# Moving x's fourth tile and the sample rows behind the first quarter of the modulation, and the gates' weights behind the last, in a one-layer hybrid decoder step

## The chip, the cores and the metric

The kernel runs on one core of a Trainium2 chip. The metric is the device time of one execution in microseconds (us); the time of the kernel before is the median of three runs. Engines are named as in the profile: PE is TensorE (PEld its weight loads), DVE is VectorE, ACT is ScalarE, POOL is GpSimd, SP is SyncE, which here only issues transfers.

## What is computed

One layer over 512 prompt rows and 64 sample rows (8 sequences of 8) of width 1024. Only its head matters here. Everything is float32.

```python
mod = silu(c) @ w_mod + b_mod                 # c: 1 prompt row and 8 sample rows; w_mod: 1024 x 6144
sh1, sc1, g1, sh2, sc2, g2 = split(mod, 6)
u = rmsnorm(x, n_pre1) * (1 + sc1) + sh1      # 576 rows
z = u @ w_in                                  # 1024 x 3072: xr, yg, q, k, v, g
...                                           # RG-LRU on xr (its gates: w_rgate, w_igate), retention on q, k, v
x = x + g1 * rmsnorm(concat(out_a, out_b) @ w_out, n_post1)
...                                           # router, 16 experts, second residual
```

## The kernel before, in words

Each engine runs its own instruction stream, written out by hand; semaphores join them. There is no scheduler: what stands ahead in an engine's stream is done first, and a wait holds up all that stands behind it.

**Tokens and tiles.** The 576 rows are five tiles t of x: 0 to 3 are 128 prompt rows each, 4 is the 64 sample rows. Each tile is squared and summed on ACT (`Square`, then `Sqrt`), scaled on DVE (`norm_x`: a reciprocal and a multiplication into `xn`), turned by PE in eight 128-column pieces into two PSUM banks (`turn_x`, line 741), and copied to `uT` (features on partitions, 8 slices k of 128 features by 576 tokens) by `take_x` on ACT (slices 0 to 3) and on DVE (slices 4 to 7).

**Scale and shift.** `1 + sc1` and `sh1` are needed per feature. They are made in four quarters q of 256 features (two slices k each). For a quarter, `scale_part(q, 0)` and `scale_part(q, 1)` on PE multiply the nine conditioning rows by two 1 MB pieces of `w_mod`, spread over four groups of 32 rows; ACT copies the first result to `part`, DVE the second; `scale_sum(q, 0)` and `(q, 1)` on PE (rows `con,arena 128x32`) add up the groups with `part` as the stationary operand; DVE makes `scaleT` from it (lines 1811, 1812, 1814) and raises `s_scaled`. Then ACT scales slice 2q of `uT` over the 512 prompt tokens (`s_uTa`), DVE slice 2q+1 (line 1821) and the sample columns of both slices (lines 1825 and 1826), raising `s_uTd` for each.

**First products.** `first_tile(q, n, m)` adds quarter q's share (slices 2q and 2q+1) to output tile m (0 to 2) of the first 512 columns of `w_in`, for token half n: 0 is tokens 0 to 287, 1 is tokens 288 to 575. It writes bank 2+2m+n. Six tiles and two parts of the next quarter make up one quarter of PE's stream; in the loop over q the next quarter's `scale_part` stand between the first three tiles and the last three, and its `scale_sum` between `first_tile(q, 1, 0)` and `(q, 1, 1)`, so that the ACT and DVE steps of a quarter lie beside products of the quarter before.

**Transfers.** SP issues, in this order: the four prompt tiles of x (512 KB each), the sample rows (256 KB), then for each quarter two pieces of `w_mod` (1 MB each, `load`, line 499) and 512 KB of `w_in` (`load_first`, line 505; it first waits until ACT has squared tile q), then the other pieces into a ring of nine 1 MB slots, each when PE has used up what the slot held. POOL issues small parameters, waits until PE has done four scale parts, issues the gates' weights (`wgate`, four transfers of 64 KB with rows of 256 bytes, line 577), waits for eight, and issues biases, norms and the rest of the constants. `wgate` is first read by `gate_products(0)`, after the 24 first tiles and `by_channel(0, 3)`.

```python
            for q in range(3):
                for m in range(3):
                    first_tile(q, 0, m)
                scale_part(q + 1, 0)
                scale_part(q + 1, 1)
                first_tile(q, 1, 0)
                scale_sum(q + 1, 0)
                scale_sum(q + 1, 1)
                first_tile(q, 1, 1)
                first_tile(q, 1, 2)
```

## Time and profile before

| | us |
|---|---|
| median of three runs | 573.47 (573.0 to 574.8) |
| the profiled execution's own time | 574.29 |
| its span in the profile | 572.3 |
| PE busy | 550.2 (96%) |
| DVE, ACT, POOL busy | 212.0 (37%), 166.4 (29%), 98.5 (17%) |

The span runs from the first instruction to the last; some 2 us lie around it. All times below are counted from the span's start. A busy share says little by itself: what counts is which engine waits, where, and for whom.

### The profile page before, as it was taken

Reading aid. Unit: us, or ns where it says so; the run is one execution under the profiler, and the core shown is the slowest. Engines: PE = TensorE matmul, PEld = TensorE weight load, DVE = VectorE, ACT = ScalarE, POOL = GpSimd, SP = SyncE. Lnnn points to the kernel's source line nnn. Section 1 sums busy time; section 2 is a strip of 40 time slices with the busy share of each in tenths; the row PEclk is TensorE's granted clock in tenths of the full one; section 3 lists DMA queues with packets and bytes.
Section 4 is the critical chain, followed back from the end, with each engine's and each line's share of the span. In section 5 each row is a group of like instructions: output and inputs, shape, how many; then the busy total and the mean of one; then the engine's idle time right before and its main releaser. Section 6 shows DMA issues by size and latency. Waiting matters only on the chain.

```text
span 572.3 us, 6747 instructions
## 1 busy us (share of the span) xinstructions
PE 550.2 (96%) x2562; PEld 341.4 (60%) x2562; DVE 212.0 (37%) x526; ACT 166.4 (29%) x326; POOL 98.5 (17%) x116
## 2 busy tenths in 40 slices
PE   7899999999999999999999999799999999999984
PEld 6577755544454555574444455677777777777641
DVE  3434386421232233325433656422223223221137
ACT  7332676712123122322323343111112112111142
POOL 3016000133000000003100211313232422232110
PEclk8999999999999999999999999999999999999998
DMA  8999997899300000089400359969999999999564
GB/s 278 356 332 338 333 351 318 296 389 340 133 1 0 0 1 1 1 286 350 118 37 37 111 177 314 274 229 340 338 326 344 354 349 332 331 354 344 125 203 166
DMA packets 73492, 133.15 MB, mean 233 GB/s; under 512 B 4138, under 2 KB 49618, under 8 KB 71410
## 3 DMA queue, kind: packets, MB, share of 16 engines
q1 hardware_dynamic: 58864, 99.36, 50.3%
q0 software_dynamic: 9536, 28.75, 18.1%
q10 hardware_dynamic: 5058, 4.58, 2.4%
q8 instruction: 22, 0.36, 0.3%
q14 instruction: 12, 0.10, 0.0%
HBM read 117.47 MB, written 18.35 MB: 237 GB/s over the span
## 4 chain that ended last, share of the span: by engine, by line
PE 87%; DVE 5%; DMA 4%; ACT 2%; issue 1%; ACTq 0%; SPq 0%
PE psum L717 82%; PE psum L720 4%; DMA ring<-in_w_mod_dram 2%; DMA out_dram<-arena 1%; DVE arena L2203 1%; ACT arena L1365 1%; DVE x L2207 1%; DMA hy<-in_c_sample_dram 1%; DVE arena L2044 0%; ACT L1365 0%; DVE arena L2125 0%; DVE arena L2258 0%; ACT ss L1365 0%; ACTq L1605 0%; ACT hy L1365 0%
## 5 line engine op out<-in xcount | busy, mean ns | idle before, releaser
L717 PE MATMUL psum<-ring,arena 128*128 128x256 f32 (+1 forms) x640 | 173.5, 427 | 1.8 <-DVE arena L2258 1.3
L717 PEld LDWEIGHTS psum<-ring,arena 128*128 128x128 f32 x640 | 120.3, 192 | 38.8 <-issue 25.8
L717 PE MATMUL psum<-ring,uT 128*128 128x512 f32 (+1 forms) x384 | 126.5, 522 | 0.0
L1365 ACT ACTIVATE arena<-psum 128x512 f32<-128x512 f32 (+6 forms) x111 | 50.7, 478 | 229.8 <-PE psum L717 202.8
L717 PEld LDWEIGHTS psum<-ring,uT 128*128 128x128 f32 (+1 forms) x384 | 56.5, 172 | 60.1 <-issue 55.8
L717 PE MATMUL psum<-uT,ring 128*128 128x288 f32 x256 | 64.9, 410 | 1.3 <-ACT uT L1365 1.3
L717 PEld LDWEIGHTS psum<-uT,ring 128*128 128x128 f32 x256 | 47.7, 190 | 17.5 <-issue 5.1
L720 PEld LDWEIGHTS psum<-con,arena 128*128 128x128 f32 (+1 forms) x295 | 35.5, 145 | 21.4 <-issue 14.1
L720 PE MATMUL psum<-con,arena 128*128 128x128 f32 (+1 forms) x295 | 42.2, 280 | 4.1 <-DVE arena L2303 3.1
L2303 DVE TENSOR_TENSOR arena<-arena,psum 128x256 f32<-128x256 f32 x16 | 6.7, 421 | 98.5 <-ACT arena L1365 98.5
L1365 ACT ACT_TABLE_LOAD x33 | 42.3, 1283 | 3.1 <-issue 2.1
L717 PE MATMUL psum<-arena 128*128 128x128 f32 (+5 forms) x188 | 35.0, 367 | 0.9 <-issue 0.7
L717 PE MATMUL psum<-ring,hy 128*128 128x512 f32 (+1 forms) x80 | 32.9, 600 | 0.5 <-ACT arena L1365 0.5
L717 PE MATMUL psum<-ring,outbT 128*128 128x512 f32 (+1 forms) x80 | 32.4, 593 | 0.0
L664 POOL DMA_INDIRECT arena<-u_dram,slot_tok x16 | 17.1, 1068 | 76.5 <-DVE slot_tok L2184 76.2
L717 PEld LDWEIGHTS psum<-arena 128*128 128x128 f32 (+3 forms) x188 | 21.3, 178 | 12.4 <-issue 10.6
L692 POOL DMA_INDIRECT f_dram<-arena,add_tok x15 | 23.9, 1596 | 18.1 <-issue 12.9
L2267 DVE TENSOR_SCALAR arena<-psum,arena 128x512 f32<-128x512 f32 x15 | 11.3, 751 | 41.7 <-PE psum L717 41.7
L1365 ACT ACTIVATE arena<-psum,con 128x128 f32<-128x128 f32 x36 | 10.4, 367 | 53.1 <-PE psum L717 46.2
L1365 ACT ACTIVATE arena<-psum,arena 128x512 f32<-128x512 f32 x15 | 10.3, 687 | 47.5 <-PE psum L717 47.5
L717 PE MATMUL psum<-ring,rowsT 128*32 128x256 f32 (+1 forms) x256 | 22.8, 490 | 0.8 <-DMA ring<-in_w_mod_dram 0.7
L717 PEld LDWEIGHTS psum<-ring,outbT 128*128 128x128 f32 (+1 forms) x80 | 13.2, 179 | 17.2 <-issue 17.2
(214 smaller groups left out, 421.8 us busy)
## 6 DMA issues: line engine op xcount, KB each, us to landing
ring<-in_w_mod_dram SPq DMA_DIRECT2D x24, 1024.0 KB, 11.4
ring<-in_w_exp_gate_dram SPq DMA_DIRECT2D x16, 1024.0 KB, 10.9
ring<-in_w_exp_up_dram SPq DMA_DIRECT2D x16, 1024.0 KB, 16.6
ring<-in_w_exp_down_dram SPq DMA_DIRECT2D x16, 1024.0 KB, 11.7
ring<-in_w_in_dram SPq DMA_DIRECT2D x10, 1024.0 KB, 14.3
ring<-in_w_out_dram SPq DMA_DIRECT2D x4, 1024.0 KB, 14.9
f_dram<-in_consts_dram POOLq DMA_DIRECT2D x1, 3072.0 KB, 20.5
arena<-in_state_ret_dram POOLq DMA_DIRECT2D x6, 512.0 KB, 5.4
```

The lines of the kernel that those rows point to most:

```text
L664: pool.indirect_dma_start(out=xg[e % 2], out_offset=None, in_=u2_dram, in_offset=bass.IndirectOffsetOnAxis(ap=slot_tok[:, e:e + 1], axis=0))\
L692: pool.indirect_dma_start(out=f_dram, in_=eo[e % 2], in_offset=None, compute_op=ALU.add, out_offset=bass.IndirectOffsetOnAxis(ap=add_tok[: ...
L717: return nc.tensor.matmul(out, lhsT, rhs, start=first, stop=last)
L720: return nc.tensor.transpose(out, src, ident[0:src.shape[0], 0:src.shape[0]])
L1365: return nc.scalar.activation(out, src, func, **kw).then_inc(done, 1)
L2203: v.scalar_tensor_tensor(out=Y[:, t, 0:w], in0=src[:, 0:w], scalar=ss[:, 3, t, 0:1], in1=tab["g2" + tag(t)][:, 0:w], op0=ALU.mult, op1=ALU ...
L2207: v.tensor_tensor(out=x[:, t, 0:w], in0=x[:, t, 0:w], in1=Y[:, t, 0:w], op=ALU.add)\
L2267: v.tensor_scalar(eo[e % 2][:, 512:1024], bank[5], gsl[e % 2][:, e:e + 1], None, ALU.mult).then_inc(s_eod, 1)
L2303: v.tensor_tensor(out=hg[e % 2], in0=hb[e % 2], in1=bank[e % 2][:, FE:2 * FE], op=ALU.mult).then_inc(s_hm, 1)
```

## The change

- SP issues tiles 0 to 2 of x, quarter 0's two pieces of `w_mod`, then tile 3 and the sample rows, then the first quarter of `w_in` and the rest as before.
- ACT and DVE norm, scale and take tiles 0 to 2 first; tile 3 and the sample rows (t = 3 and 4) are normed after quarter 0's scale is applied to tokens 0 to 383, and then taken and scaled over tokens 384 to 511 in instructions of their own. ACT takes all eight slices of the sample rows.
- PE does quarter 0's first three tiles (token half 0), then turns tiles 3 and 4, and does `scale_part(1, 0)` after `first_tile(0, 1, 0)`, and `scale_part(1, 1)` and both sums of quarter 1 after `first_tile(0, 1, 2)`. Quarters 2 and 3 keep their order.
- POOL issues the gates' weights after eight scale parts, ahead of the biases.

```diff
--- before.py
+++ after.py
@@ -507,14 +507,18 @@
                              w_in[0, q * 2 * P:(q + 1) * 2 * P, 0:512]
                              .rearrange("(k p) n -> p k n", p=P)).then_inc(s_xt[q], 16)
-            for t in range(TILES - 1):
+            def load_x(t):
                 sp.dma_start(x[:, t, :], x_prompt[0, t * P:(t + 1) * P, :]).then_inc(s_xt[t], 16)
-            sp.dma_start(x[0:NS, TILES - 1, :], x_sample.rearrange("b t d -> (b t) d"))\
-                .then_inc(s_xt[TILES - 1], 16)
-
+
+            for t in range(TILES - 2):
+                load_x(t)
             for q in range(4):
                 load(("scale", q, 0))
                 load(("scale", q, 1))
+                if q == 0:
+                    load_x(TILES - 2)
+                    sp.dma_start(x[0:NS, TILES - 1, :], x_sample.rearrange("b t d -> (b t) d"))\
+                        .then_inc(s_xt[TILES - 1], 16)
                 load_first(q)
             for p in weight_pieces():
                 if p[0] != "scale" and p[:2] != ("in", 0) and p not in late:
@@ -570,13 +574,12 @@
             pool.dma_start(brow[16:24, :], norm_pre_mix[0].rearrange("(r n) -> r n", n=P))\
                 .then_inc(s_par, 16)
-            pool.wait_ge(s_scale, 4)
+            pool.wait_ge(s_scale, 8)
             for gi, w in enumerate((w_rgate, w_igate)):
                 wv = w[0].rearrange("(m a) j k -> a j m k", a=2)
                 for a in range(2):
                     pool.dma_start(wgate[64 * a:64 * a + 64, gi, :, :], wv[a]).then_inc(s_par, 16)
-            pool.wait_ge(s_scale, 8)
             pool.wait_ge(s_clear, 3)
             for j in range(4):
                 pool.dma_start(bm[32 * j:32 * j + 32, :, :],
@@ -741,11 +744,14 @@
                 n = rows(t)
                 pe.wait_ge(s_xn, t + 1)
                 if t >= 3:
-                    pe.wait_ge(s_rawa, t - 2)
-                    pe.wait_ge(s_rawd, t - 2)
-                b = 2 + 2 * (t % 3)
+                    pe.wait_ge(s_rawd, t - 1)
                 for k in range(KT):
-                    at = bank[b + k // 4][:, (k % 4) * P:(k % 4) * P + n]
+                    if t < 3:
+                        at = bank[2 + 2 * t + k // 4][:, (k % 4) * P:(k % 4) * P + n]
+                    elif t == 3:
+                        at = bank[3 + 2 * (k // 4)][:, (k % 4) * P:(k % 4) * P + n]
+                    else:
+                        at = bank[7][:, k * n:(k + 1) * n]
                     last = turn(at, xn[0:n, t, k * P:(k + 1) * P])
                 last.then_inc(s_uTp, 1)
@@ -777,10 +783,8 @@
             turn_x(2)
             turn_rows()
             scale_part(0, 0)
-            turn_x(3)
+            scale_sum(0, 0)
             scale_part(0, 1)
-            turn_x(4)
-            scale_sum(0, 0)
             scale_sum(0, 1)
             half = NTOK // 2
@@ -813,18 +817,30 @@
                 w = ring[:, slot["in", 0, q // 2], :].rearrange("p (k n) -> p k n", n=512)
                 if m == 0 and n == 0:
                     pe.wait_ge(s_xt[q], 32)
-                    pe.wait_ge(s_uTa, q + 1)
+                    pe.wait_ge(s_uTa, q + 1 + (q > 0))
                 if m == 0 and n == 1:
-                    pe.wait_ge(s_uTd, 2 * q + 2)
+                    pe.wait_ge(s_uTa, q + 2)
+                    pe.wait_ge(s_uTd, 2 * q + 3)
                 for k in (2 * q, 2 * q + 1):
                     if m == 0 and n == 0 and k % 2 == 1:
-                        pe.wait_ge(s_uTd, 2 * q + 1)
+                        pe.wait_ge(s_uTd, 2 * q + 1 + (q > 0))
                     last = mm(bank[2 + 2 * m + n][:, 0:half], w[:, k % 4, m * P:(m + 1) * P],
                               uT[:, k, n * half:(n + 1) * half], k == 0, k == KT - 1)
                 if q == 3 and n == 1:
                     last.then_inc(s_xr, 1)
-            for q in range(3):
+            for m in range(3):
+                first_tile(0, 0, m)
+            turn_x(3)
+            turn_x(4)
+            first_tile(0, 1, 0)
+            scale_part(1, 0)
+            first_tile(0, 1, 1)
+            first_tile(0, 1, 2)
+            scale_part(1, 1)
+            scale_sum(1, 0)
+            scale_sum(1, 1)
+            for q in (1, 2):
                 for m in range(3):
                     first_tile(q, 0, m)
                 scale_part(q + 1, 0)
@@ -1377,33 +1393,50 @@
             def take_x(t):
                 n = rows(t)
                 act.wait_ge(s_uTp, t + 1)
-                b = bank[2 + 2 * (t % 3)][:].rearrange("p (k i) -> p k i", i=P)
-                f(uT[:, 0:4, t * P:t * P + n], b[:, :, 0:n], ACT.Copy, s_rawa)
-
-            for t in range(TILES):
+                if t < TILES - 1:
+                    b = bank[2 + 2 * t if t < 3 else 3][:].rearrange("p (k i) -> p k i", i=P)
+                    f(uT[:, 0:4, t * P:t * P + n], b[:, :, 0:n], ACT.Copy, s_rawa)
+                else:
+                    b = bank[7][:].rearrange("p (k i) -> p k i", i=n)
+                    f(uT[:, :, t * P:t * P + n], b, ACT.Copy, s_rawa)
+
+            def size_x(t):
                 n = rows(t)
                 act.wait_ge(s_xt[t], 16)
                 f(xn[0:n, t], x[0:n, t], ACT.Square, s_sq, accum_out=ss[0:n, 0, t, 0:1])
                 act.wait_ge(s_sq, t + 1)
                 f(ss[0:n, 0, t, 0:1], ss[0:n, 0, t, 0:1], ACT.Sqrt, s_xrms, scale=1.0 / D,
                   bias=eps[0:n, 0:1])
-                if t >= 2:
-                    take_x(t - 2)
+
+            size_x(0)
+            size_x(1)
+            size_x(2)
+            take_x(0)
+            take_x(1)
+            take_x(2)
+
+            def times_scale(k, tokens):
+                f(uT[:, k, tokens], uT[:, k, tokens], ACT.Identity, s_uTa,
+                  scale=scaleT[:, 0, k, 0:1], bias=scaleT[:, 1, k, 0:1])
             def scale_u(q):
                 act.wait_ge(s_scale, 2 * q + 1)
                 if q:
                     act.wait_ge(s_scaleT, 2 * q)
                 f(part[:, 0, 0:256], bank[0][:, 0:256], ACT.Copy, s_parta)
-                if q == 0:
-                    take_x(TILES - 2)
-                    take_x(TILES - 1)
                 act.wait_ge(s_scaled, q + 1)
-                if q == 0:
-                    act.wait_ge(s_rawa, TILES)
-                    act.wait_ge(s_rawd, TILES)
-                f(uT[:, 2 * q, 0:SEQ], uT[:, 2 * q, 0:SEQ], ACT.Identity, s_uTa,
-                  scale=scaleT[:, 0, 2 * q, 0:1], bias=scaleT[:, 1, 2 * q, 0:1])
+                if q:
+                    times_scale(2 * q, slice(0, SEQ))
+                    return
+                act.wait_ge(s_rawa, 3)
+                act.wait_ge(s_rawd, 3)
+                times_scale(0, slice(0, 3 * P))
+                size_x(3)
+                size_x(4)
+                take_x(3)
+                take_x(4)
+                act.wait_ge(s_rawa, TILES)
+                times_scale(0, slice(3 * P, SEQ))
             scale_u(0)
             scale_u(1)
@@ -1783,7 +1816,7 @@
             def take_x(t):
                 n = rows(t)
                 dve.wait_ge(s_uTp, t + 1)
-                b = bank[3 + 2 * (t % 3)][:].rearrange("p (k i) -> p k i", i=P)
+                b = bank[3 + 2 * t if t < 3 else 5][:].rearrange("p (k i) -> p k i", i=P)
                 v.tensor_copy(uT[:, 4:KT, t * P:t * P + n], b[:, :, 0:n]).then_inc(s_rawd, 1)
             norm_x(0)
@@ -1791,10 +1824,8 @@
             take_x(0)
             norm_x(2)
             take_x(1)
-            norm_x(3)
             take_x(2)
             take_rows()
-            norm_x(4)
             def scale_u(q):
@@ -1802,24 +1833,36 @@
                 of = lambda j: bank[j][:, 0:64].rearrange("p (k r) -> p k r", r=32)[:, :, 0:1 + DB]
                 wide = lambda r: r.unsqueeze(2).to_broadcast([P, 2, 1 + DB])
                 a, b = scaleT[:, 0, two, 0:1 + DB], scaleT[:, 1, two, 0:1 + DB]
-                dve.wait_ge(s_scale, 2 * q + 2)
-                v.tensor_copy(part[:, 1, 0:256], bank[1][:, 0:256]).then_inc(s_partd, 1)
-                if q == 0:
-                    take_x(TILES - 2)
-                    take_x(TILES - 1)
+                if q:
+                    dve.wait_ge(s_scale, 2 * q + 2)
+                    v.tensor_copy(part[:, 1, 0:256], bank[1][:, 0:256]).then_inc(s_partd, 1)
                 dve.wait_ge(s_scaleT, 2 * q + 1)
                 link(v.tensor_tensor(out=a, in0=of(0), in1=wide(biasT[:, 1, two]), op=ALU.add))
                 link(v.tensor_tensor(out=a, in0=a, in1=wide(biasT[:, 2, two]), op=ALU.mult))
+                if q == 0:
+                    dve.wait_ge(s_scale, 2)
+                    v.tensor_copy(part[:, 1, 0:256], bank[1][:, 0:256]).then_inc(s_partd, 1)
                 dve.wait_ge(s_scaleT, 2 * q + 2)
                 v.tensor_tensor(out=b, in0=of(1), in1=wide(biasT[:, 0, two]), op=ALU.add)\
                     .then_inc(s_scaled, 1)
                 dve.wait_ge(s_scaled, q + 1)
+                k = 2 * q + 1
+
+                def times_scale(tokens):
+                    v.tensor_scalar(uT[:, k, tokens], uT[:, k, tokens], scaleT[:, 0, k, 0:1],
+                                    scaleT[:, 1, k, 0:1], ALU.mult, ALU.add).then_inc(s_uTd, 1)
+
                 if q == 0:
-                    dve.wait_ge(s_rawd, TILES)
+                    dve.wait_ge(s_rawd, 3)
+                    dve.wait_ge(s_rawa, 3)
+                    times_scale(slice(0, 3 * P))
+                    norm_x(3)
+                    norm_x(4)
+                    take_x(3)
                     dve.wait_ge(s_rawa, TILES)
-                k = 2 * q + 1
-                v.tensor_scalar(uT[:, k, 0:SEQ], uT[:, k, 0:SEQ], scaleT[:, 0, k, 0:1],
-                                scaleT[:, 1, k, 0:1], ALU.mult, ALU.add).then_inc(s_uTd, 1)
+                    times_scale(slice(3 * P, SEQ))
+                else:
+                    times_scale(slice(0, SEQ))
                 each = lambda j: scaleT[:, j, two, 1:1 + DB].unsqueeze(3).to_broadcast([P, 2, DB, DT])
                 u = uT[:, two, SEQ:NTOK].rearrange("p k (b t) -> p k b t", t=DT)
                 link(v.tensor_tensor(out=u, in0=u, in1=each(0), op=ALU.mult))
```

PE's stream from quarter 0's first scale part to quarter 1's first products. Names: `ring,rowsT 32x256` are scale parts (x8 is one), `con,arena 128x128` and `128x64` the turns of a prompt tile and of the sample rows, `con,arena 128x32` the sums (x2 is one), `uT,ring 128x288` first tiles (x2 is one). Before:

```order
L717 MATMUL psum<-ring,rowsT 32x256 x8
L720 MATMUL psum<-con,arena 128x128 x8
L717 MATMUL psum<-ring,rowsT 32x256 x8
L720 MATMUL psum<-con,arena 128x64 x8
L717 MATMUL psum<-con,arena 128x32 x4
L717 MATMUL psum<-uT,ring 128x288 x6
L717 MATMUL psum<-ring,rowsT 32x256 x16
L717 MATMUL psum<-uT,ring 128x288 x2
L717 MATMUL psum<-con,arena 128x32 x4
L717 MATMUL psum<-uT,ring 128x288 x10
```

And in the changed kernel:

```order
L720 MATMUL psum<-con,arena 128x32 x2
L720 MATMUL psum<-ring,rowsT 32x256 x8
L720 MATMUL psum<-con,arena 128x32 x2
L720 MATMUL psum<-uT,ring 128x288 x6
L723 MATMUL psum<-con,arena 128x128 x8
L723 MATMUL psum<-con,arena 128x64 x8
L720 MATMUL psum<-uT,ring 128x288 x2
L720 MATMUL psum<-ring,rowsT 32x256 x8
L720 MATMUL psum<-uT,ring 128x288 x4
L720 MATMUL psum<-ring,rowsT 32x256 x8
L720 MATMUL psum<-con,arena 128x32 x4
L720 MATMUL psum<-uT,ring 128x288 x6
```

The turns moved from before the sums to behind three first tiles, quarter 1's parts moved behind `first_tile(0, 1, 0)` and `(0, 1, 2)`, and its sums from between the products to behind them all.

ACT's stream over the same stretch (`arena,ss<-x` is a tile's square, `ss<-ss,eps` its root, `uT<-psum` take_x, `arena<-psum 128x256` the copy of a part, `uT<-uT,scaleT` the scaling of a slice). Before:

```order
L1365 ACTIVATE uT<-psum 128x4x128 [waits s_uTp]
L1365 ACTIVATE arena,ss<-x 64x1024 [waits s_xt4]
L1365 ACTIVATE ss<-ss,eps 64x1 [waits s_sq]
L1365 ACTIVATE uT<-psum 128x4x128 [waits s_uTp]
L1365 ACTIVATE arena<-psum 128x256 [waits s_scale]
L1365 ACTIVATE uT<-psum 128x4x128 [waits s_uTp]
L1365 ACTIVATE uT<-psum 128x4x64 [waits s_uTp]
L1365 ACTIVATE uT<-uT,scaleT 128x512 [waits s_rawd,s_rawa,s_scaled]
L1365 ACTIVATE arena<-psum 128x256 [waits s_scaleT,s_scale]
L1365 ACTIVATE uT<-uT,scaleT 128x512 [waits s_scaled]
```

And in the changed kernel:

```order
L1381 ACTIVATE uT<-psum 128x4x128 [waits s_uTp] x3
L1381 ACTIVATE arena<-psum 128x256 [waits s_scale]
L1381 ACTIVATE uT<-uT,scaleT 128x384 [waits s_rawd,s_rawa,s_scaled]
L1381 ACTIVATE arena,ss<-x 128x1024 [waits s_xt3]
L1381 ACTIVATE ss<-ss,eps 128x1 [waits s_sq]
L1381 ACTIVATE arena,ss<-x 64x1024 [waits s_xt4]
L1381 ACTIVATE ss<-ss,eps 64x1 [waits s_sq]
L1381 ACTIVATE uT<-psum 128x4x128 [waits s_uTp]
L1381 ACTIVATE uT<-psum 128x8x64 [waits s_uTp]
L1381 ACTIVATE uT<-uT,scaleT 128x128 [waits s_rawa]
L1381 ACTIVATE arena<-psum 128x256 [waits s_scaleT,s_scale]
L1381 ACTIVATE uT<-uT,scaleT 128x512 [waits s_scaled]
```

The squares and takes of tiles 3 and 4 moved from ahead of the first scaling to behind it, and the copy of quarter 1's first part now stands behind all of them.

## Rows read from the trace of the kernel before

**Rows 1.** The page, part 4: the chain that ended last, shares of the span by engine.

```profile
PE 87%; DVE 5%; DMA 4%; ACT 2%; issue 1%; ACTq 0%; SPq 0%
```

**Rows 2.** The chain in order of time: start, length, what.

```profile
26.36 90.77 PE psum L717 x540
```

**Rows 3.** Timeline, PE and PEld: start, length, engine, line, what, [idle before <-releaser].

```profile
7.90 0.66 PE L720 MATMUL psum<-con,hy 9*128 9x9 f32 x8 [1.56 <-DMA con<-in_consts_dram]
...
15.31 1.07 PE L717 MATMUL psum<-ring,rowsT 128*32 128x256 f32 x16
...
16.31 1.09 PE L720 MATMUL psum<-con,arena 128*128 128x128 f32 x8
...
18.47 0.71 PE L720 MATMUL psum<-con,arena 64*128 64x64 f32 x8
...
19.11 1.08 PE L717 MATMUL psum<-con,arena 128*128 128x32 f32 x8
...
21.47 3.15 PE L717 MATMUL psum<-uT,ring 128*128 128x288 f32 x12 [1.28 <-ACT uT L1365]
...
26.36 1.07 PE L717 MATMUL psum<-ring,rowsT 128*32 128x256 f32 x16 [0.74 <-DMA ring<-in_w_mod_dram]
...
27.36 1.24 PE L717 MATMUL psum<-uT,ring 128*128 128x288 f32 x4
...
29.25 5.10 PE L717 MATMUL psum<-uT,ring 128*128 128x288 f32 x20
...
34.27 2.01 PE L717 MATMUL psum<-ring,rowsT 128*32 128x256 f32 x32
...
35.21 0.59 PEld L717 LDWEIGHTS psum<-ring,rowsT 128*32 128x32 f32 x16 [0.35 <-DMA ring<-in_w_mod_dram]
...
62.57 2.17 PE L717 MATMUL psum<-arena,wgate 64*64 64x512 f32 x16
```

**Rows 4.** Timeline, ACT and DVE, same columns.

```profile
12.51 1.05 ACT L1365 ACTIVATE arena<-x 128x1024 f32<-128x1024 f32 x1
...
13.68 0.29 ACT L1365 ACTIVATE ss<-ss,eps 128x1 f32<-128x1 f32 x1
...
14.27 0.75 DVE L1780 TENSOR_SCALAR arena<-x,ss 128x1024 f32<-128x1024 f32 x1
...
15.72 0.57 ACT L1365 ACTIVATE uT<-psum 128x512 f32<-128x512 f32 x1
...
18.61 0.42 DVE L1806 COPY arena<-psum 128x256 f32<-128x256 f32 x1 [1.48 <-PE psum L717]
...
19.88 0.17 DVE L1811 TENSOR_TENSOR scaleT<-psum,rowsT 128x18 f32<-128x18 f32 x1
...
20.51 0.82 ACT L1365 ACTIVATE uT<-uT,scaleT 128x512 f32<-128x512 f32 x1 [0.91 <-DVE scaleT L1814]
...
21.29 0.29 DVE L1826 TENSOR_TENSOR uT<-uT,scaleT 128x128 f32<-128x128 f32 x1
...
29.73 0.81 ACT L1365 ACTIVATE uT<-uT,scaleT 128x512 f32<-128x512 f32 x1 [3.66 <-DVE scaleT L1814]
```

**Rows 5.** Two-microsecond windows: busy of each engine, granted clock, DMA share, GB/s.

```profile
10.00:12.00 2.00, 1.99 (x10) 1.99 (x11) 0.92 (x2) 1.64 (x5) 0.00 (x0) 0.50 1.11 256
20.00:22.00 2.00, 0.72 (x4) 0.57 (x4) 1.44 (x6) 0.82 (x1) 0.00 (x0) 1.00 1.11 351
32.00:34.00 2.00, 2.00 (x10) 1.52 (x8) 1.14 (x7) 1.55 (x3) 0.00 (x0) 1.00 1.11 273
34.00:36.00 2.00, 2.00 (x34) 0.83 (x32) 0.78 (x6) 0.38 (x1) 0.00 (x0) 1.00 1.07 244
```

**Rows 6.** Tile ring, SP, from 28.7 us: scale piece (3, 1), issue to landing.

```profile
L499 SPq DMA_DIRECT2D ring<-in_w_mod_dram x1: 3318/3318/3318, 28.7 to 28.7; - x1
...
DMA to landing us min/median/max: 14.2/14.2/14.2
```

**Rows 7.** The page, part 6 and the DMA view: the gates' weights, median us to landing.

```profile
wgate<-in_w_rgate_dram POOLq DMA_DIRECT2D x2, 64.0 KB, 5.8
```


## The prediction

> **What bounds the kernel now.** First the chain of waits by engine: 87% of the span is PE, 4% DMA [rows 1]. Then the same chain in order of time: from 26.36 us on it is PE's own stream, 540 instructions without a foreign step [rows 2]. So past 26.36 a microsecond of PE idle time, added or removed, goes to the end, unless a transfer or another engine stands in between. Third, the timeline of PE around the change: what bounds it there is read from the brackets. After quarter 0's sums PE idles 1.28 us until ACT has scaled the first slice, and 0.74 us at 26.36 until piece (1, 1) of w_mod has landed [rows 3]. The next piece that it waits for is (2, 1), and that wait shows only on the weight load, 0.35 us at 35.21 [rows 3]. Piece (3, 1) lands at 28.7 + 14.2 = 42.9 us [rows 6], before PE reads it (PE comes to it one quarter, some 9 us, after 35.21). So up to 26.36 transfers set the pace, and from there PE is just barely ahead of being held by them.
>
> The DMA engines are full there (share over 1, 351 GB/s), and at 32 to 36 us they carry only 273 and 244 GB/s [rows 5]: that is when the gates' weights land, issued from 27.8 us in rows of 256 bytes, 5.8 us to landing [rows 7].
>
> **The change, part by part.** The anchor is the start of first_tile(1, 0, 0). Before, the 20 records from 29.25 us are five first tiles of 1.02 us each (5.10 / 5) [rows 3], of which two belong to quarter 0: it starts at 29.25 + 2.04 = 31.3 us. From it on both kernels have the same order on PE.
>
> *Start.* Tiles 0 to 2 are loaded, normed and turned as before; quarter 0's part (0, 0) again starts at 15.31, behind the turned parameter rows, for 1.07 us [rows 3]. Its weights had come by then even with 768 KB more ahead of them.
>
> *Quarter 0's scale.* Part (0, 0) ends at 16.4; the copy (like DVE's, 0.42 us [rows 4]) to 16.9; the first sum takes PE half of 1.08 us, to 17.4; part (0, 1) to 18.5 [rows 3]. DVE's copy, 0.42 us, to 19.0; the sum starts at 19.1. Before, DVE read a sum 0.77 us after its start (19.11 to 19.88), and ACT's scaling began 0.63 us later, behind three DVE instructions of some 0.2 us each [rows 3, 4]; now two of the three are done earlier. So ACT starts at 19.1 + 0.8 + 0.2 = 20.1, not 20.51. It scales 384 columns: 512 took 0.82 us, I take 0.65. First products at 20.8 instead of 21.47 us: 0.7 won.
>
> *Tiles 3 and 4, now in the open.* Three first tiles, 3.15 us [rows 3], end at 23.95. Beside them ACT squares tile 3 (20.75; root 1.17 us later, as 12.51 to 13.68, and 0.29 long) and tile 4 (22.1; root ends at 23.6); DVE's reciprocal and multiplication (0.15 + 0.75) give tile 4 at 24.6 [rows 4]. Up to here all is hidden. Then PE turns tile 3 (1.09 us, the next may start after 0.85) and tile 4 (0.71) [rows 3], ending at 25.5. What follows is on the path, since first_tile(0, 1, 0) waits for both: ACT takes tile 3 (0.57) from 25.1 and tile 4, now eight slices, 512 columns, also 0.57, from 25.7, to 26.3 [rows 4]; then DVE, which waits for ACT here, scales 128 columns (0.25, from 0.55 for 512) and does the two sample instructions, 0.29 each [rows 4]. That is 27.2; PE resumes at 27.3 after 1.8 us of idle time. Before, first_tile(0, 1, 0) started at 27.36 [rows 3]. The two kernels are level there, but before had already done parts (1, 0) and (1, 1), and now both still stand ahead.
>
> *Quarter 1's scale, in the open too.* first_tile(0, 1, 0) 1.02, part (1, 0) 0.95 (34.27 to 35.21, one part behind the other [rows 3]), two first tiles 2.04, part (1, 1) 1.07: 27.3 + 5.1 = 32.4 us. All of w_mod it needs landed by 26.3. Now nothing is left of quarter 0 to lie beside the handing over: DVE's copy from 32.45 to 32.9, the second sum 0.8 to 33.7, line 1814 0.2, ACT's scaling of 512 columns 0.81 (29.73 [rows 4]): 34.7, and PE at 34.8 us. Of those 2.4 us PE works about 1.0 on the sums. Before, scaling ended at 30.54 and PE came to it at 31.3: hidden whole.
>
> So the anchor moves from 31.3 to 34.8: **+3.5 us**. Back comes what PE lost at 35.21 to piece (2, 1): two parts took 2.01 us [rows 3] against 2 x 0.95, so 0.1. Sum: **+3.4 us**.
>
> *The gates' weights.* Away from 32 to 36 us they free the DMA engines: 4 us at a mean of 258 GB/s instead of 351 [rows 5] is 0.37 MB not moved, and 0.26 MB of what was moved was theirs, together 0.63 MB or 1.8 us for pieces (3, 1) and what follows, some 1.3 us for (2, 1), which was landing. But with PE at 37.9 us for part (2, 0), (2, 1) landed before 35.2 and (3, 1) before 42.9, no transfer is waited for: worth nothing. The Trainium skill, DMA: Bandwidth & Descriptors, Why small descriptors are slow, gives a 256-byte descriptor 27% overhead; by that the 256 KB would cost about 1.0 us and not 1.8, an estimate by that page. It changes neither term above. Later the four issues, 0.65 us each by the issue times, start when PE has done eight parts, at about 48.8, ahead of the biases; with 5.8 us to landing [rows 7], and 10 as a bound for fuller queues, they land by 62. They are read at 62.57 + 3.4 = 66 us [rows 3]. The biases and norms slip 3 us and are read after the first eight mod steps, tens of microseconds later.
>
> *The rest of the kernel* is PE's stream, its transfers released by PE itself, and so moves as a whole.
>
> Against the median of 573.47, +3.4 gives **576.9 us** (the profiled execution was 574.29, span 572.3: those would be 577.7 and 575.7). The unknowns: the 384-, 128- and 512-column instructions that the trace lacks, and some ten handoffs of 0.05 to 0.1 us; 0.9 us either way. A measurement tells about 0.3%, 1.7 us, from no change.
>
> **Rivals.**
>
> *Transfers go on setting the pace, and PE is not late (not slower).* If the copies and scalings overlapped so well that quarter 0's last tiles ran before 26.3 us, part (1, 1) would start on its landing as before, and the three first tiles that followed it would be done. Then (2, 1) is the next wait, and it lands up to 1.3 us earlier without the gates' weights: 572.2 us. For it: PE did wait at 26.36 and 35.21 for just these pieces. Against: it decides if first_tile(0, 1, 0) starts before 22.3 us (three tiles and part (1, 0) ahead of 26.3), and PE ends only the first three tiles at 23.95, with work it cannot drop. A half of it, in which the two open handoffs shrink by 1.5 to 2 us together, ends near 575. I give 12% to results under 575.2, of which 3% to a gain over 1.7 us.
>
> *The clock.* After 1.56 us of idle time at 6.34 to 7.90 and then only small turns, the granted clock was 0.50 over 10 to 12 us, which is 1.2 GHz; at 20 to 22 us, with PE busy 0.72 of 2 us, it stayed at 1.00, 2.4 GHz [rows 3, 5]. The new gaps of 1.8 and 1.4 us stand between dense work, as the latter did. If one did lower it for 3.5 us, as around 9 to 13, half of that is lost: 1.75 more, 578.7 us. The Trainium skill, TensorE: Matmul & The Clock Gate, HAM oscillation, names such idle gaps between loads as what halves the clock; its example's gaps are longer than these, and beyond the two rows above no row shows what a gap as short as these does. This case has 8%.
>
> *The gates' weights come too late.* If they took as long as the constants that now stand behind them, near 18 us, they would land at 69.5, and PE would stand 3.5 us more at 66: 580.4 us. Against: they are first in POOL's queue. 3%.
>
> **How the numbers follow.** The forecast, 77%: 575.2 to 577.9. Under 575.2: 12%. The clock 8%, the weights 3%. The range from 574.6 to 578.7 leaves out about 6% below and 7% above. Slower by over 0.3%: 77 + 8 + 3 = 88%, less 2 for the forecast's own edge, 86%; within 0.3%: 11%; faster: 3%.
>
> **What would show it.** Right: PE's first products start near 20.8; an idle time near 1.8 us before first_tile(0, 1, 0) at 27.3, ended by DVE's sample instruction; one of some 1.4 us before first_tile(1, 0, 0) at 34.8, ended by ACT's scaling; parts (2, 0) and (2, 1) at 37.9 with no wait on a transfer; the gate products at 66. Wrong: quarter 1's part (1, 1) before 28 us; a granted clock under 1.00 after 13 us; a wait on `wgate`; or parts of quarter 2 still waiting for w_mod, which would mean that transfers, and not the order, set the pace.

## The result, and the profile after

| | before | changed |
|---|---|---|
| median of four runs each, us | 574.13 (573.00 to 574.85) | 581.72 (577.85 to 583.61) |
| profiled execution, its span | 574.29, 572.3 | 577.85, 575.9 |

The medians lie 7.6 us apart (1.3%); the ratio on record is 1.0098, with an interval from 1.0066 to 1.013, which is 5.6 us. By either the change is slower, by 1.7 to 2.2 times the 3.4 us forecast, and the median is outside the range. The profiled execution was the quickest of the changed kernel's four, and 0.95 us from the forecast. So two things want explaining: what this trace shows, and what the three other executions, at 581.4 to 583.6, had besides. The mean granted clock gives the first hint: 0.990 in the profiled one, and 0.987, 0.985 and 0.982 in those of 581.4, 582.05 and 583.6 us.

The page of the changed kernel: busy time by engine, chain by engine.

```profile
PE 550.0 (96%) x2562; PEld 341.1 (59%) x2562; DVE 212.1 (37%) x526; ACT 167.8 (29%) x327; POOL 98.2 (17%) x116
...
PE 86%; DVE 6%; DMA 5%; ACT 1%; issue 1%; ACTq 0%; POOLq 0%; DVEq 0%
```

PE is as busy as before (550.0 against 550.2 us) and its share of the chain is about the same, 86% against 87% [rows 1]: no work was added. Its place in time changed: it waited more (below), and where the clock was low the same products took longer. The timeline of PE (start, length, engine, line, operation, tiles, count, idle time before and what ended it) answers to [rows 3]:

```profile
14.72 1.07 PE L720 MATMUL psum<-ring,rowsT 128*32 128x256 f32 x16
...
18.54 0.63 PE L720 MATMUL psum<-con,arena 128*128 128x32 f32 x4 [0.62 <-DVE arena L1844]
...
20.28 4.84 PE L720 MATMUL psum<-uT,ring 128*128 128x288 f32 x12 [1.11 <-ACT uT L1381]
...
28.33 1.21 PE L720 MATMUL psum<-uT,ring 128*128 128x288 f32 x4 [1.69 <-DVE uT L1869]
...
29.46 1.07 PE L720 MATMUL psum<-ring,rowsT 128*32 128x256 f32 x16
...
32.60 1.07 PE L720 MATMUL psum<-ring,rowsT 128*32 128x256 f32 x16
...
36.14 3.15 PE L720 MATMUL psum<-uT,ring 128*128 128x288 f32 x12 [1.28 <-ACT uT L1381]
...
39.21 1.93 PE L720 MATMUL psum<-ring,rowsT 128*32 128x256 f32 x32
```

And ACT and DVE, answering to [rows 4]:

```profile
19.43 0.71 ACT L1381 ACTIVATE uT<-uT,scaleT 128x384 f32<-128x384 f32 x1 [3.19 <-DVE scaleT L1846]
...
27.31 0.50 ACT L1381 ACTIVATE uT<-uT,scaleT 128x128 f32<-128x128 f32 x1
...
27.89 0.29 DVE L1869 TENSOR_TENSOR uT<-uT,scaleT 128x128 f32<-128x128 f32 x1
...
35.17 0.82 ACT L1381 ACTIVATE uT<-uT,scaleT 128x512 f32<-128x512 f32 x1 [4.19 <-DVE scaleT L1846]
```

The gap structure is the predicted one: 1.69 us of idle time ahead of first_tile(0, 1, 0), ended by DVE's sample instruction (predicted 1.8), and 1.28 us ahead of first_tile(1, 0, 0), ended by ACT's scaling (predicted 1.4); parts (2, 0) and (2, 1) without a wait on a transfer. The first products began at 20.28, 0.5 us ahead of the forecast, because part (0, 0) had itself started at 14.72 and not at 15.31; from that part to the products it is 5.6 us, where 5.5 was reckoned. But the first products took 4.84 us for the same 12 records that took 3.15 [rows 3], and with these 1.69 us more (4.84 less 3.15) first_tile(1, 0, 0) starts at 36.14 instead of 34.8. Two-microsecond windows (busy of PE, PEld, DVE, ACT, POOL, granted clock, DMA share, GB/s) say why; a granted clock of 1.00 is 2.4 GHz, 0.50 is 1.2 GHz, and values between are windows in which it changed:

```profile
19.00:21.00 2.00, 0.89 (x5) 0.71 (x5) 0.66 (x2) 1.57 (x3) 0.00 (x0) 1.00 1.11 350
21.00:23.00 2.00, 2.00 (x7) 1.36 (x6) 1.01 (x3) 1.81 (x6) 0.00 (x0) 0.56 1.08 345
23.00:25.00 2.00, 2.00 (x7) 1.38 (x6) 0.81 (x2) 0.00 (x0) 0.00 (x0) 0.59 1.07 373
25.00:27.00 2.00, 1.64 (x17) 1.33 (x15) 0.69 (x1) 0.92 (x2) 0.00 (x0) 1.00 1.10 350
```

At 21 to 25 us the granted clock is 0.56 and 0.59: it fell to 1.2 GHz at 21.2 and came back at 24.6. Before it fell, in 19 to 21 us, PE was busy 0.89 of 2 us. In the kernel before, with 0.72 busy in 20 to 22, it had stayed at 1.00 [rows 5]. The gate products came at 67.4 us, 4.8 later than before [rows 3], but the end only 3.6 later: in the kernel before the clock also fell at 371 us, behind the 2.2 us gap ahead of the first expert's turn, and in this execution of the changed kernel it did not. PE before:

```profile
369.45 0.44 PE L720 MATMUL psum<-con,arena 128*128 128x128 f32 x2 [2.21 <-DVE arena L2303]
370.25 8.83 PE L717 MATMUL psum<-ring,arena 128*128 128x256 f32 x32 [0.36 <-DVE arena L2258]
```

and in the changed kernel:

```profile
374.94 7.14 PE L720 MATMUL psum<-ring,arena 128*128 128x256 f32 x32 [0.37 <-DVE arena L2301]
```

So past 13 us each of the two profiled executions lost about 1.7 us to one such stretch (4.84 against 3.15, 8.83 against 7.14), the changed kernel at 21 us and before at 371. The two cancel, and the 3.6 us that are left are the order. That this execution came out beside the forecast is therefore luck in part: the forecast held neither stretch.

### The profile page after: what moved, and what is told of

Same layout as the page of the kernel before. It is cut to its first block, busy times and chain, and to the rows that moved or that the text cites. A ratio compares the mean times of both kernels' runs of the same rounds, so it can differ in the third digit from the quotient of the medians.

```text
span 575.9 us, 6751 instructions
## 1 busy us (share of the span) xinstructions
PE 550.0 (96%) x2562; PEld 341.1 (59%) x2562; DVE 212.1 (37%) x526; ACT 167.8 (29%) x327; POOL 98.2 (17%) x116
## 4 chain that ended last, share of the span: by engine, by line
PE 86%; DVE 6%; DMA 5%; ACT 1%; issue 1%; ACTq 0%; POOLq 0%; DVEq 0%
PE psum L720 80%; PE psum L723 5%; DMA f_dram<-arena,add_tok 2%; DMA out_dram<-arena 1%; DVE arena L2246 1%; DMA con<-in_consts_dram 1%; DVE x L2250 1%; DMA arena<-f_dram 1%; ACT arena L1381 1%; ACT uT L1381 0%; DVE arena L2087 0%; DVE arena L2168 0%; DVE arena L2375 0%; DVE arena L2301 0%; ACTq L1638 0%
## 5 line engine op out<-in xcount | busy, mean ns | idle before, releaser
L720 PEld LDWEIGHTS psum<-ring,arena 128*128 128x128 f32 x640 | 119.1, 190 | 38.3 <-issue 25.8
L720 PE MATMUL psum<-uT,ring 128*128 128x288 f32 x256 | 66.9, 418 | 4.1 <-ACT uT L1381 2.4
L720 PE MATMUL psum<-ring,outbT 128*128 128x512 f32 (+1 forms) x80 | 32.4, 593 | 0.0
L720 PEld LDWEIGHTS psum<-arena 128*128 128x128 f32 (+3 forms) x188 | 21.2, 178 | 12.8 <-issue 10.6
L684 POOL DMA_INDIRECT arena<-gates_dram,slot_tok x15 | 14.5, 970 | 49.3 <-DVE arena L2310 22.2
```

The source lines that it names most:

```text
L684: pool.indirect_dma_start(out=gsl[e % 2], out_offset=None, in_=gates_dram, in_offset=bass.IndirectOffsetOnAxis(ap=slot_tok[:, e:e + 1], ax ...
L720: return nc.tensor.matmul(out, lhsT, rhs, start=first, stop=last)
```

## The experiments

All ran with the kernel before beside them on the same chip. Its median there was 575.2, 574.8 and 575.5 us in the three sets, with executions from 571.5 to 578.7: wider than the first runs had shown. "Filler" means a product of the identity matrix with 128 columns (itself or a table of constants) into PSUM columns that nobody reads, in a place where PE is idle anyway. Theory C is that the new order costs what was forecast and that the clock's falls are the rest. Theory O is that the order is all, and the rest is scatter.

**1. The changed kernel again (after_again)**, with no edit.

> The changed kernel once more, in the same runs as the others. Theory C (the new order of PE costs some 3 us, and the gaps it opens before 29 us let the granted clock fall to 0.50 once more, 1.7 us each time): the median stays 577 to 583 us, the mean clock lies under that of the kernel before (0.991) by about 0.003 for each extra low stretch, and the time rises with it; the profile shows a stretch at 0.50 between 15 and 40 us in which first tiles take 1.6 us instead of 1.05. Rival O (the order alone, the rest being scatter of the chip): 576 to 578 us, and clock and time are not tied.

Measured: 583.8 us (577.6 to 585.3), before 575.2; ratio 1.0117 (1.0068 to 1.0166). The profiled execution was a long one, 584.85 us, clock 0.982. Its windows, as above:

```profile
19.00:21.00 2.00, 1.32 (x3) 1.07 (x4) 0.38 (x2) 1.97 (x5) 0.00 (x0) 0.50 1.10 353
21.00:23.00 2.00, 2.00 (x5) 1.43 (x5) 1.51 (x4) 1.24 (x3) 0.00 (x0) 0.50 1.10 353
23.00:25.00 2.00, 2.00 (x5) 1.38 (x5) 0.24 (x1) 0.00 (x0) 0.00 (x0) 0.50 1.08 369
...
29.00:31.00 2.00, 2.00 (x4) 0.97 (x4) 0.00 (x0) 0.00 (x0) 0.00 (x0) 0.50 1.10 350
39.00:41.00 2.00, 2.00 (x6) 1.37 (x5) 0.85 (x5) 1.96 (x4) 0.00 (x0) 0.51 1.05 385
```

and PE's rows where the clock was low:

```profile
19.68 5.96 PE L720 MATMUL psum<-uT,ring 128*128 128x288 f32 x12 [1.10 <-ACT uT L1381]
...
28.84 2.26 PE L720 MATMUL psum<-uT,ring 128*128 128x288 f32 x4 [1.69 <-DVE uT L1869]
...
38.24 4.84 PE L720 MATMUL psum<-uT,ring 128*128 128x288 f32 x12 [1.28 <-ACT uT L1381]
```

The clock was low from 18.5 to 25.4, 28.8 to 32.2 and 39.0 to 42.4 us, and once more from 380.3 to 383.8, behind the gap ahead of the first expert's turn. The first products take 5.96, first_tile(0, 1, 0) 2.26 instead of 1.21, quarter 1's first three tiles 4.84, and first_tile(1, 0, 0) starts at 38.24. The six executions fall in order: 577.6 and 579.5 at clocks of 0.993 and 0.990, the four of 583.0 to 585.3 at 0.979 to 0.982, about 1.65 us for each 0.003. The two profiled executions of this kernel give much the same account. From part (0, 0), at 14.12 here and 14.72 in the first, to the end they took 568.7 and 561.2 us, 7.5 apart. In that time this one was at the low clock for 17.1 us and the first for 3.4 (the end of the span left out), and half of the 13.7 us between them is 6.8. Theory C holds, O does not, though the median lies 0.8 over C's range. What was wrong in C as written is "once more": it can be several times. The Trainium skill, TensorE: Matmul & The Clock Gate, What's actually happening, says that the gate's observation runs freely and does not start with the kernel, so that the same program meets it at another point each time. The traces agree: the same kernel lost the clock at 21.2 us in one execution and at 18.5, 28.8 and 39.0 in the other.

**2. Fillers in the changed kernel's gaps (warm_start).**

```diff
             scale_part(0, 0)
+            pe.wait_ge(s_rawd, 3)
+            pe.wait_ge(s_rawa, 3)
+            fill(3)                       # mm(bank[7][:, 0:P], ident, ident)
             scale_sum(0, 0)
             scale_part(0, 1)
+            fill(4)
             scale_sum(0, 1)
+            fill(7)
...
             turn_x(4)
+            pe.wait_ge(s_scaled, 1)
+            fill(11, 0)                   # into bank 0
             first_tile(0, 1, 0)
...
             scale_sum(1, 1)
+            pe.wait_ge(s_scaled, 2)
+            fill(5, 0)                    # into bank 0
```

> The changed kernel with small products into PSUM columns that nobody reads, put into PE's gaps before the first sums (3 and 4), behind them (7), ahead of first_tile(0, 1, 0) (11) and of first_tile(1, 0, 0) (5). PE's order and its real work stay. Theory C: the granted clock stays at 1.00 from 15 to 60 us, first_tile(1, 0, 0) starts near 34.5 us, the median is 576 to 578.5, that is 2 to 5 us under the changed kernel, and the runs lie closer together. Rival O: the fillers change nothing or cost up to 1 us; same median as the changed kernel.

Measured: 579.4 us (578.5 to 581.8) against 583.8 of the same kernel without fillers on the same chip: 4.4 us less by work added, and a spread of 3.3 instead of 7.7 us. These are seven and six executions and their ranges overlap; the ratios to before, 1.0082 (1.005 to 1.0113) and 1.0117, are 2.0 us apart. So the size is rough, and the trace carries the reading. The windows show why:

```profile
19.00:21.00 2.00, 2.00 (x17) 1.90 (x17) 0.64 (x2) 1.77 (x4) 0.00 (x0) 1.00 1.09 350
21.00:23.00 2.00, 2.00 (x10) 1.58 (x9) 1.21 (x4) 1.61 (x4) 0.00 (x0) 1.00 1.10 352
23.00:25.00 2.00, 2.00 (x20) 1.61 (x18) 1.20 (x2) 0.59 (x1) 0.00 (x0) 1.00 1.07 368
...
29.00:31.00 2.00, 2.00 (x18) 1.30 (x11) 0.00 (x0) 0.38 (x1) 0.00 (x0) 1.00 1.10 352
```

No low stretch from 15 to 375 us; one of 3.4 us came at 375.5, ahead of the first expert, where this kernel had no filler. The fillers were too many (one is some 0.25 us, not the 0.14 of a turned piece), so first_tile(1, 0, 0) came at 35.5 and not 34.5, and the median lies 0.9 above the expected range. 4.2 us over before remained.

**3. Quarter 1's parts and sums back in before's place (q1_early).**

```diff
             turn_x(4)
-            first_tile(0, 1, 0)
             scale_part(1, 0)
-            first_tile(0, 1, 1)
-            first_tile(0, 1, 2)
             scale_part(1, 1)
+            first_tile(0, 1, 0)
             scale_sum(1, 0)
             scale_sum(1, 1)
+            first_tile(0, 1, 1)
+            first_tile(0, 1, 2)
```

> The changed kernel with quarter 1's two parts back ahead of first_tile(0, 1, 0) and its sums back behind it, as before; tiles 3 and 4 stay behind the first quarter. If the open handoff of quarter 1 and the parts that came behind the gap are what costs: the two parts fill the gap ahead of first_tile(0, 1, 0) and the scaling is hidden again, so the anchor, first_tile(1, 0, 0), is back at 31 to 32 us and the median at 573 to 575. Rival (the turn of tiles 3 and 4 behind the first tiles is itself the cost, since their norms and takes come late): 576 or more, with an idle time over 1 us left ahead of first_tile(0, 1, 0).

Measured: 575.6 us (573.1 to 578.7), ratio to before 1.0013 (0.999 to 1.0036): the loss is gone, with tiles 3 and 4 still behind the first quarter. (Median and anchor lie 0.6 and 0.5 us over the expected ranges, before itself being at 575.2.)

```profile
20.40 4.84 PE L720 MATMUL psum<-uT,ring 128*128 128x288 f32 x12 [1.10 <-ACT uT L1381]
...
26.68 1.93 PE L720 MATMUL psum<-ring,rowsT 128*32 128x256 f32 x32
28.55 1.24 PE L720 MATMUL psum<-uT,ring 128*128 128x288 f32 x4
...
30.43 5.10 PE L720 MATMUL psum<-uT,ring 128*128 128x288 f32 x20
```

The two parts at 26.68 fill what was the 1.69 us gap, and no idle time is left ahead of first_tile(0, 1, 0) at 28.55, so the rival falls. first_tile(1, 0, 0) starts at 30.43 + 2.04 = 32.5, although this execution too had one low stretch (the 4.84 at 20.40). The clock still falls; what the order of quarter 1 adds is gone.

**4. Only the gates' weights moved (wgate_late).** POOL waits for eight parts instead of four ahead of them, nothing else differs from before.

> The kernel before with only the gates' weights issued after eight scale parts. Prediction: the DMA engines carry about 350 GB/s at 32 to 36 us, piece (2, 1) lands before PE comes to it, PE gains 0.1 us there and the median is within 0.3% of before (573 to 574.5). Rival: the biases and norms behind them come too late for their reader and the kernel is slower by 1 us or more; or the freed DMA time is worth its 1.3 us, 572.

Measured: 576.3 us (572.6 to 578.0), ratio 1.0004 (0.9981 to 1.0027): no difference to before, as predicted, though the 573 to 574.5 written down was missed.

```profile
20.00:28.00 8.00, 6.72 (x22) 4.80 (x22) 2.21 (x8) 1.18 (x2) 0.00 (x0) 0.57 1.09 355
...
32.00:34.00 2.00, 2.00 (x9) 1.53 (x9) 1.21 (x4) 1.76 (x2) 0.00 (x0) 1.00 1.09 357
34.00:36.00 2.00, 2.00 (x10) 1.58 (x9) 0.85 (x5) 1.96 (x4) 0.00 (x0) 1.00 1.10 348
```

```profile
18.24 1.07 PE L716 MATMUL psum<-ring,rowsT 128*32 128x256 f32 x16 [0.91 <-DMA ring<-in_w_mod_dram]
...
19.88 1.28 PE L716 MATMUL psum<-con,arena 128*128 128x32 f32 x8
...
22.44 5.62 PE L716 MATMUL psum<-uT,ring 128*128 128x288 f32 x12 [1.28 <-ACT uT L1364]
```

The DMA engines carry 357 and 348 GB/s at 32 to 36 us instead of 273 and 244 [rows 5]. This bears out the reading that the weights' transfers caused the dip; by bytes it was 1.8 us of DMA time, an estimate from these windows, not the 1.0 that the prediction worked out by the Trainium skill, DMA: Bandwidth & Descriptors, Why small descriptors are slow. It was worth next to nothing, since PE waited for piece (2, 1) by 0.35 us at most, on a weight load [rows 3]. The first row matters more: with PE's order of before, the clock was low from 20.6 to 27.4 us. It fell during the sums, which took 1.28 us instead of 1.08, behind a 0.91 us wait for part (0, 1) and ahead of the 1.28 us gap of [rows 3], which lies at 21.2 to 22.4 here. So "it stayed at 1.00 there" was true of one execution and not of the kernel.

**5. Only quarter 1's late order, in the kernel before (q1_late_only).**

```diff
-            for q in range(3):
+            for m in range(3):
+                first_tile(0, 0, m)
+            first_tile(0, 1, 0)
+            scale_part(1, 0)
+            first_tile(0, 1, 1)
+            first_tile(0, 1, 2)
+            scale_part(1, 1)
+            scale_sum(1, 0)
+            scale_sum(1, 1)
+            for q in (1, 2):
```

> The kernel before with only PE's order of quarter 1 changed as in the changed kernel: part (1, 0) behind first_tile(0, 1, 0), part (1, 1) and both sums behind first_tile(0, 1, 2). Theory C, order: first products at 21.5 us (full clock), no wait for piece (1, 1) any more, but the open handoff of 1.3 us; first_tile(1, 0, 0) at 32.1, that is 0.8 us later than before at the same clock; median 573.5 to 577 with before at 575. Rival (the late order of quarter 1 alone is the loss): 577 to 579, first_tile(1, 0, 0) at 34 us or later with the clock at 1.00.

Measured: 578.5 us (575.5 to 580.6) against 574.8; ratio 1.0067 (1.0043 to 1.0091).

```profile
21.28 5.59 PE L717 MATMUL psum<-uT,ring 128*128 128x288 f32 x16 [1.28 <-ACT uT L1374]
...
33.46 4.84 PE L717 MATMUL psum<-uT,ring 128*128 128x288 f32 x12 [1.28 <-ACT uT L1374]
```

It lost 3.6 us, over theory C's range and inside the rival's; but the rival wanted the clock at 1.00, and it was not. By its trace, 33.46 for first_tile(1, 0, 0) is 2.2 later than before; 1.4 of that is the low clock in the first products (5.59 for four tiles; at 1.02 to 1.05 us each they take 4.2), and 0.8 is left, as reckoned. But the clock fell again at 34.4, behind the open handoff: quarter 1's tiles take 4.84. In this execution, the only one profiled, the order alone cost about what was reckoned, and two low stretches (from 20.8 and from 34.4 us) cost the rest.

**6 to 8. Fillers in other orders (before_warm, mix_warm, q1_early_warm).** before_warm is the kernel before with 5 fillers behind quarter 0's sums, 3 ahead of part (1, 1), and 8 ahead of the first expert's turn; mix_warm has first_tile(0, 1, 0) in place of the 3 and the late gates' weights; q1_early_warm is experiment 3 with 2, 2, 5 and 8.

```diff
             scale_sum(0, 1)
+            pe.wait_ge(s_rawa, 3)
+            pe.wait_ge(s_rawd, 3)
+            fill(5)
...
                 scale_part(q + 1, 0)
+                if q == 0:
+                    fill(3)
                 scale_part(q + 1, 1)
...
+                    if e == 0:
+                        pe.wait_ge(s_snew, 1)
+                        keep_running(8, 5)
                     turn_hidden(e)
```

> The kernel before with small products into unread PSUM columns in three gaps of PE: 5 behind quarter 0's sums, 3 ahead of part (1, 1), 8 ahead of the first expert's turn (where PE idles 2.2 us near 368). Theory C: executions of the kernel before differ by where its clock falls, so with the gaps filled the granted clock is 1.00 from 15 to 560 us, mean 0.993 or more, and the median is 1.5 to 4 us under before, 571.5 to 573.5, with less scatter. Rival (the scatter is not the clock's, or the fillers delay real work as much as the clock does): within 1 us of before.

> As the one before it (fillers of 5 and of 8), with the gates' weights after eight parts, and first_tile(0, 1, 0) between part (1, 0) and part (1, 1) instead of fillers there, so that the wait for piece (1, 1) holds a product. Expected: first_tile(1, 0, 0) at 30.7 us instead of 31.3, median 0.5 to 1 us under before_warm, 571 to 573. Rival: piece (2, 1) or the handoffs take it back, and it equals before_warm.

> The changed kernel with quarter 1's parts and sums back in before's place, and fillers of 2, 2, 5 and 8. Theory C: with the clock at 1.00, first_tile(1, 0, 0) starts at 30.8 us (it was 32.5 with one low stretch of 3.4 us), so tiles 3 and 4 behind the first quarter are worth 0 to 0.5 us by themselves; median 571 to 573, as mix_warm. Rival: 575, as without fillers.

Measured, with before at 574.8: before_warm 574.1 (572.1 to 574.9), ratio 0.9975 (0.9957 to 0.9993); mix_warm 574.9 (574.0 to 577.9), 1.0013 (0.9994 to 1.0032); q1_early_warm 573.9 (572.6 to 575.2), 0.9976 (0.9958 to 0.9994). The 35 executions of before in this set, by mean clock: ten at 0.992 or more with a median of 573.4, ten at 0.990 or 0.991 with 574.8, nine at 0.987 to 0.989 with 575.1, six below with 577.6. So before's scatter goes with the clock in good part, and the fillers mainly take the longest executions away (highest 574.9 instead of 578.7); the median gains 0.7 to 0.9 us, half or less of what was expected. q1_early_warm is 0.2% faster than before in this set; its repetition below, at 0.9986, does not tell it from before. mix_warm did not do what was expected of it, though it reached first_tile(1, 0, 0) at 30.6 us.

**9 to 12. The order at full clock, and mix_warm's loss.** after_warm is the changed kernel with fillers of 2, 2, 5, 7, 3 and 8; it and q1_early_warm_2 (the kernel of experiment 8) differ only in quarter 1's order and the fillers of 7 and 3 that its gaps need. before_warm_wgate_late and mix_warm_wgate_early exchange only the place of the gates' weights.

> The changed kernel in its own order, with fillers fitted to the gaps (2, 2, 5, 7, 3, and 8 ahead of the first expert's turn), to be set against q1_early_warm_2 on the same chip: the two then differ only in where quarter 1's two parts and sums stand. Theory C: clock 1.00 from 15 to 60 us, first_tile(1, 0, 0) at 34.5 to 35 against 31.4, and a median 3.0 to 3.8 us over q1_early_warm_2, about 577. Rival (the clock made up nearly all of the loss, and the order is covered): within 1 us of it.

> The same kernel as q1_early_warm, beside the others of this call: 573 to 574.5 us, 1 to 1.5 us under before.

> before_warm with only the gates' weights after eight parts. At a steady clock: if the 0.1 us at piece (2, 1) is all there is to win, 574 us, within 0.5 us of q1_early_warm_2 and of the earlier 574.1 of before_warm. Rival: the late weights cost something that shows once the clock is out of the way, 575 or more.

> mix_warm with the gates' weights back behind four parts. mix_warm reached first_tile(1, 0, 0) at 30.6 us, 1.3 us ahead of before_warm, and was yet 0.8 us slower by its median. If the late gates' weights take that back, this kernel is at 572.5 to 573.5. Rival (it is the order, or the scatter of that chip): 574.5 to 575.5 again.

Measured, with before at 575.5: after_warm 576.6 (575.2 to 577.9), ratio 1.0012 (0.9993 to 1.0032); q1_early_warm_2 574.0 (572.9 to 575.2), 0.9986 (0.9965 to 1.0008); before_warm_wgate_late 573.3 (572.2 to 575.8), 0.998 (0.9961 to 0.9999); mix_warm_wgate_early 575.0 (573.7 to 577.3), 1.0 (0.9979 to 1.002). PE in after_warm:

```profile
20.29 3.15 PE L720 MATMUL psum<-uT,ring 128*128 128x288 f32 x12
...
26.64 1.21 PE L720 MATMUL psum<-uT,ring 128*128 128x288 f32 x4
...
30.92 1.07 PE L720 MATMUL psum<-ring,rowsT 128*32 128x256 f32 x16
31.92 1.25 PE L720 MATMUL psum<-con,arena 128*128 128x32 f32 x8
...
34.44 3.15 PE L720 MATMUL psum<-uT,ring 128*128 128x288 f32 x12
```

and in q1_early_warm_2:

```profile
26.74 1.07 PE L720 MATMUL psum<-ring,rowsT 128*32 128x256 f32 x16 [1.22 <-DMA ring<-in_w_mod_dram]
...
29.62 5.10 PE L720 MATMUL psum<-uT,ring 128*128 128x288 f32 x20
```

At full clock first_tile(1, 0, 0) starts at 34.44 in the changed order and at 29.62 + 2.04 = 31.7 in the other, 2.8 us apart; the medians are 2.6 apart (3.0 to 3.8 was expected), and the twelve executions of each hardly overlap (575.2 is the lowest of one and the highest of the other). By the ratios to before it is 1.5 us. With the fillers, those ahead of the first expert among them, the changed kernel is at 576.6 us, 5 to 7 under its own medians without them on other chips, and within 0.2% of before. The second row of q1_early_warm_2 shows what its early start met: 1.22 us of waiting for piece (1, 1), so that part (1, 1) starts at 26.74, against 26.36 in [rows 3]; moving tiles 3 and 4 had nothing to win there.

That pair prices quarter 1's order alone. The whole change of order is the difference between after_warm and before_warm_wgate_late, which share chip, late gates' weights and a full clock from 15 us on. PE in the latter:

```profile
26.82 1.24 PE L716 MATMUL psum<-uT,ring 128*128 128x288 f32 x4
...
28.70 5.10 PE L716 MATMUL psum<-uT,ring 128*128 128x288 f32 x20
```

They are level at first_tile(0, 1, 0), 26.64 and 26.82, and 3.7 us apart at first_tile(1, 0, 0), 34.44 and 28.70 + 2.04 = 30.7. The medians are 3.3 apart, the profiled executions 3.5, and only one of the twelve executions of before_warm_wgate_late lies above any of after_warm. (The ratios to before, 1.0012 and 0.998, put it at 1.8 us.) Of the 3.3, 0.75 lie between before_warm_wgate_late and q1_early_warm_2, and the latter is the slower one: moving tiles 3 and 4 won nothing.

mix_warm_wgate_early is as slow as mix_warm, so the gates' weights did not take its gain. Its gain is gone near the end. In mix_warm's last stage, where expert results are read back from f_dram and summed, PE waits 1.16 us for DVE (1.71 in mix_warm_wgate_early) and 0.54 for a transfer:

```profile
554.38 2.13 PE L716 MATMUL psum<-arena 128*64 128x512 f32 x6 [1.16 <-DVE arena L2350]
557.05 1.12 PE L716 MATMUL psum<-arena,con 128*128 128x512 f32 x2 [0.54 <-DMA arena<-f_dram]
```

q1_early_warm_2 does the first stretch in one run of 14 records, without the wait for DVE (its wait for f_dram is 0.36):

```profile
549.71 5.85 PE L720 MATMUL psum<-arena 128*128 128x512 f32 x14
```

From the last expert's tokens (507 us in both) to the end mix_warm took 65.7 and q1_early_warm_2 63.8 us. Other executions show 63 to 66 us there, whatever the head of the kernel. Why both mix kernels met the longer ones was not settled.

## Why the prediction was wrong

- **The sum of the order, +3.4 us, was right.** At full clock the changed order is 3.3 us slower in the medians, and first_tile(1, 0, 0) starts 3.7 us later (after_warm against before_warm_wgate_late) or 3.1 later than in the execution of before that the forecast was read from. Quarter 1's order makes 2.6 of it. Predicted and found in after_warm: first products at 20.8 and 20.29, first_tile(0, 1, 0) at 27.3 and 26.64, part (1, 1) ending at 32.4 and 31.99, first_tile(1, 0, 0) at 34.8 and 34.44, gate products at 66 and 65.7.
- **Level at first_tile(0, 1, 0), then two parts behind:** right, 26.64 against 26.82; experiment 3 undoes just that, and the kernel is level with before.
- **The rival that transfers go on setting the pace** fell: parts (2, 0) and (2, 1) of the changed kernel waited for none, and part (1, 1) ran at 32.60, long after 28.
- **Quarter 1's handoff in the open:** right, 1.28 us of idle time against 1.4.
- **The gates' weights worth nothing:** right (experiment 4), and their 1.8 us of DMA time is borne out. The rival that they come too late fell: no wait on them shows in any trace.
- **The clock was the step that failed.** The sum put it at nothing, since the new gaps "stand between dense work, as the latter did"; as a rival it had 8%, one stretch and 1.75 us. The price of one stretch was right (4.84 against 3.15 us, 1.69). Its chance was not, nor its number: of the six profiled executions without fillers (before, changed, after_again, q1_early, wgate_late, q1_late_only), all but the one I had read before predicting lost the clock between 18 and 28 us, and after_again lost it at three places before 45 us. Of the eight profiled executions with fillers none lost it between 14 and 375 us. By the medians the fillers took away 4.4 of the changed kernel's 8.6 us over before on that chip; by the ratios, 2.0 of 6.7.
- **Why it failed:** I took one execution's row as the kernel's behaviour. That row stood at 1.00 behind a 1.28 us gap [rows 3, 5], and from it I argued that gaps between dense work are safe. wgate_late has that same order and gap and was 6.8 us at 1.2 GHz around it. Nor is it always the gap that goes ahead of a fall: the clock fell 0.9 us behind the end of a gap (21.2 in the changed kernel), within one (20.8 in q1_late_only) and ahead of one (18.5 in after_again, 20.6 in wgate_late). The change also took the turns of tiles 3 and 4, 1.8 us of dense work, out of the stretch ahead of the first products; that this made falls more likely is not shown, since wgate_late and q1_late_only have these turns in place and lost the clock as well.
- **The base was a favourable one too.** 573.47 was the median of three runs; in the later sets before has 574.8 to 575.5, up to 578.7. A range of 4 us, reckoned with 0.9 us of unknowns, could not hold the scatter: executions of the changed kernel ran from 577.6 to 585.3.

The fillers are products as well as warmth; that they act through the clock, and not otherwise, is shown by the windows (1.00 throughout) and by record lengths returning to 3.15, not by the medians alone. What decides when the clock falls was not tried and stays open.

## What to carry to other kernels

Where PE is the bound, price a reordering twice: by the work and the handoffs that come into the open, and by what the new gaps can do to the granted clock, and read the clock over several executions before calling a gap harmless. A handoff chain of copy, sum and scaling should have products beside it that do not depend on it; here three tiles put behind the next quarter's parts are worth 2.6 us by the medians. Where a gap must stay, a few products into unread PSUM columns, fewer than the gap holds, took away the longest executions.

## What was not expected of the hardware

The clock can be low for 6.9 us on end (18.5 to 25.4 in after_again) although PE is busy 2.00 of 2 us over the second half of it. It falls at different times in executions of one kernel, and so the mean clock, 0.979 to 0.993 for one and the same program, goes with 7 us of its scatter. And a filler of 128 columns in float32 cost 0.25 us each in a row (11 of them took 2.72 us in warm_start), where the turn of a 128-column piece costs 0.14; the trace has two records for each filler and one for each turned piece.
